# Token scales of five norms brought to all partitions by two DMAs through DRAM, and a gate chain moved by one unit

## The chip, the cores and the metric

One core of one Trainium2 chip runs the kernel. The metric is the device time of one execution in microseconds; for the kernel before it is the median of three runs, 1869.68 us (1867.63 to 1871.52).

## What is computed

A trunk of two layers on 512 tokens of width 1024, in float32. Each layer is half an FFN, a mixer, and half an FFN; each of these starts from a norm over the 1024 features of a token. The first mixer is forgetting attention, the second banded attention (windows of two chunks of 64 tokens) with sinks. A last norm follows.

```python
def rms_norm(x, g):
    xf = x.astype(F32)
    y = xf * lax.rsqrt(jnp.mean(xf * xf, axis=-1, keepdims=True) + RMS_EPS)
    return (y * g.astype(F32)).astype(x.dtype)

def swiglu(x, w_in, w_out):
    gate, up = jnp.split(x @ w_in, 2, axis=-1)
    return (jax.nn.silu(gate) * up) @ w_out

# forgetting attention: q, k, v, f_logit = split(u @ w_in)
    log_f = jax.nn.log_sigmoid((f_logit + b_f).astype(F32))
    c = jnp.cumsum(log_f, axis=1).transpose(0, 2, 1)
    s = s + cb[..., None] - c[:, :, None, :]
# banded attention: q, k, v = split(u @ w_in + b_in)

    for i in range(DEPTH):
        h = h + 0.5 * swiglu(rms_norm(h, norm_g[i, 0]), ffn_w_in[i, 0], ffn_w_out[i, 0])
        u = rms_norm(h, norm_g[i, 1])
        m = fox_mixer(u, ...) if kind == 0 else swa_mixer(u, ...)
        h = h + m
        h = h + 0.5 * swiglu(rms_norm(h, norm_g[i, 2]), ffn_w_in[i, 1], ffn_w_out[i, 1])
    return rms_norm(h, final_g)
```

## The kernel before

The residual `h` lies in SBUF with the features on partitions, 8 blocks of 128 features by 512 tokens. All products are split in three: a value is kept as a high part `_hi` (rounded) and the rest `_lo`, and a product is the matmuls hi x hi, hi x lo and lo x hi. ScalarE makes the high parts, VectorE the low ones, TensorE multiplies.

**Weights** come in units of 128 x 1024 values (512 KB), numbered through the whole program. SyncE loads them into a ring `raw` of four (`load`, L323 to L328): the load of unit n waits until unit n - 4 has been split (`w_ready`). ScalarE copies a unit into one of two `w_hi` slots once TensorE has used the unit two before (`split_next`, L1112 to L1119), VectorE makes `w_lo` (`split_lo`, L1546). A unit is 24 matmuls of 128 x 512.

**Norms** are numbered nn = 0 to 5 (FFN 0, forgetting attention 1, FFN 2 and 3, banded attention 4, FFN 5). The gain is put on `h` before the products, the scale of each token only after them, since it is a factor of a column. So a section starts with its first two units while the scale is being made: `token_sums` (L518) on TensorE, `mean_squares` (L1578) on VectorE, a power of -0.5 on GpSimd (`pow_rstd`, L453), which gives `rstd`, a token per partition, 128 x 4. What follows the products has the tokens along the row, and needs the scale as a row on all partitions, `rstd_row`. For this VectorE writes four diagonal matrices (`diagonals`, L1585), TensorE multiplies them by ones (`row_sums`, L524) into bank 5, and ScalarE copies it (`row_copy`, L1180).

**FFN** (`ffn`, `in_body`): a body is four units, two for 256 gate features (banks 0 and 1) and two for the same up features (banks 2 and 3). VectorE scales the gate by `rstd_row` (L1650), ScalarE applies SiLU (L1198), VectorE scales and multiplies the up half. TensorE's next body waits for the gate scaling (`gate_scaled`) before it takes banks 0 and 1 again. In the first body `row_sums` stands behind the third unit.

**Forgetting attention** (`fox`): unit 0 is V, unit 1 the gate logits (bank 4, 16 rows), then the rest of V (units with k = 1 to 7), with the first q and k between. The gate chain on VectorE and ScalarE (L1765 to L1818, L1320 to L1327) takes the logits, applies the row, and makes the running sum `decay`; it stands at k = 1 and 2. At k = 3 ScalarE and VectorE take the first four banks of V (`v_ready`), and TensorE's first q waits for bank 0 of them.

**Banded attention** (`window`): k and v units, then q of pair 0 and 1. `row_sums` stands after five of the eight steps of q's first unit. After the row VectorE scales k (L1951), q (L1948) and v (L1953); ScalarE and VectorE make the halves (L1440, L1423, L1431, L1909), then split the next weight unit (L1114, L1546). Then come the rounds of the head pairs: scores (L994), maxima (L1969), exponentials (L1473), normalizing (L2019), turning, values. `place_q` has SyncE move a q into place in every round, in the order of its loads.

The order on every engine is the order of the code.

Of the kernel before, what the change touches and what calls it, by code (L numbers as in the profile page):

```python
# [45 lines left out]
FIRST_AT = (11264, 10240)  # L46
LAST_PAIR = (KB // 2 - 1) * len(OUT_KBS)
# [30 lines left out]
def build(nc, x, gains, ffn_in, ffn_out, mix_w, fox_b, swa_bq, swa_bk, swa_bv, sinks, y):  # L78
    ctx = ExitStack()
    with ctx:  # L80
# [25 lines left out]
        diag = sb("diag", [P, SEQ])  # L106
        gain = sb("gain", [P, 7 * KB])
# [65 lines left out]
        row_ready = sem("row_ready")  # L173
        gate_scaled = sem("gate_scaled")
# [134 lines left out]
        def _(sp):  # L309
# [20 lines left out]
            def load_ffn(f):  # L330
# [22 lines left out]
                with sp.Fori(1, IN_BODIES) as i:  # L353
                    load_in(i)
# [16 lines left out]
            def load_window():  # L371

                for u in range(SWA_UNITS):
# [8 lines left out]
                    load((SWA_BASE + u) % RAW, mix_w[FOX_UNITS + u], UNIT, SWA_BASE + u - RAW + 1)  # L382

# [24 lines left out]
            load_ffn(0)  # L408
            load_fox()
            load_ffn(1)  # L410
            load_ffn(2)
            load_window()
            load_ffn(3)
# [77 lines left out]
        def _(pe):  # L491
# [30 lines left out]
            def row_sums(nn):  # L522
                pe.wait_ge(diag_ready, nn + 1)
# [76 lines left out]
            def ffn(f, nn):  # L600
                base = FFN_BASE[f]

                def in_body(i):
                    peeled = type(i) is int
                    for r in range(IN_UNITS):
# [17 lines left out]
                        if peeled and r == 2:  # L623
                            row_sums(nn)
# [202 lines left out]
            def fox(nn):  # L827
                n = FOX_BASE
                for k in range(V_UNITS):
# [4 lines left out]
                    if k == V_UNITS // 2:  # L834
                        pe.wait_ge(row_ready, nn + 1)
# [19 lines left out]
                    if k == 1:  # L855
                        row_sums(nn)
# [111 lines left out]
            def window(nn):  # L968
# [74 lines left out]
                row_sums(nn)  # L1043
# [63 lines left out]
        def _(act):  # L1107
# [70 lines left out]
            def row_copy(nn):  # L1178
                act.wait_ge(row_sum, nn + 1)
                act.activation(rstd_row[:, :], bank[5][:, :], ACT.Copy).then_inc(row_ready, 1)  # L1180

            def ffn(f, nn, last):
                base = FFN_BASE[f]

                def in_body(i):
                    for r in range(IN_UNITS):
# [6 lines left out]
                        if type(i) is int and r == 2:  # L1193
# [112 lines left out]
            def fox(nn):  # L1306
# [5 lines left out]
                row_copy(nn)  # L1312
                for k in range(1, V_UNITS):
                    step(n)
                    n += 1
                    if k == 1:
# [8 lines left out]
                    if k == 2:  # L1325
# [125 lines left out]
            def window(nn):  # L1451
# [5 lines left out]
                row_copy(nn)  # L1457
# [83 lines left out]
        def _(dve):  # L1541
# [84 lines left out]
            def ffn(f, nn, last):  # L1626
                base = FFN_BASE[f]

                def in_body(i):
                    first = type(i) is int  # L1630
                    for r in range(IN_UNITS):
# [7 lines left out]
                        if first and r == 1:  # L1639
                            if f == 0:  # L1640
                                first_mean_squares()
                            else:
                                mean_squares(nn, 5)
                            diagonals(nn)
                        if r == (2 if first else 1):
                            dve.wait_ge(unit_used, base + 4 * i + (3 if f == 0 and first else 2))
                            if first:
                                dve.wait_ge(row_ready, nn + 1)
# [105 lines left out]
            def fox(nn):  # L1754
# [7 lines left out]
                diagonals(nn)  # L1762
                dve.wait_ge(row_ready, nn + 1)
                dve.wait_ge(unit_used, FOX_BASE + 2)
                dve.tensor_tensor(x0, bank[4][0:HEADS, :], rstd_row[0:HEADS, :], ALU.mult).then_inc(f_chain, 1)  # L1765
                dve.wait_ge(f_chain, 1)
# [350 lines left out]
```

## Time and profile before

| | us |
|---|---|
| median of 3 runs | 1869.68 |
| the profiled execution | 1868.03 |
| its span, first to last instruction | 1866.2 |
| TensorE matmuls busy | 1849.2 (99%) |
| VectorE busy | 926.1 (50%) |
| ScalarE busy | 696.1 (37%) |
| DMA, mean of 16 engines | 97 GB/s |

The granted clock of TensorE is 0.999. The chain that ended last is followed back from the last instruction, at each step to what released it. A matmul of 128 x 512 is shown with 0.39 us, yet one begins every 0.23 us: matmuls overlap, so steps between starts are read rather than durations.

### The profile page before, as it was taken

To read this page: it belongs to the slowest core of one execution; us is meant where nothing else is said; L and a number is where in the kernel's file an instruction comes from. 1 tells how busy PE (TensorE), PEld (TensorE's weight loads), DVE (VectorE), ACT (ScalarE), POOL (GpSimd) and SP (SyncE) were. 2 spreads that over 40 slices of the span, in tenths; PEclk is the share of its full clock that TensorE was granted. 3 is DMA by queue.
4 is the path that set the end of the run, shared out by engine and by line. 5 is a ranking of instruction groups with operands and counts; after the bars stand their busy time and mean duration, and the time that the engine had idled before them with its cause. 6 is when DMAs were issued, how large, how long until landed. Compare 5 with 4: busy or idle time off the path is not lost.

```text
span 1866.2 us, 24031 instructions
## 1 busy us (share of the span) xinstructions
PE 1849.2 (99%) x8703; PEld 1522.8 (82%) x8703; DVE 926.1 (50%) x1337; ACT 696.1 (37%) x1149; POOL 24.7 (1%) x44
## 2 busy tenths in 40 slices
PE   9999999999999999999999999999999999999998
PEld 7888888877777888888888888888887888888888
DVE  5444434356887544444334444434379644444332
ACT  5232223245765432323323323323368433232332
POOL 1000000000000000000000000000000000000000
PEclk9999999999999999999999999999999999999999
DMA  4223223323332232222333232223322222222332
GB/s 170 101 91 101 87 89 105 119 95 107 86 94 67 94 102 91 100 97 81 110 107 106 96 101 90 96 88 108 122 79 70 91 93 98 99 92 90 96 104 84
DMA packets 59882, 181.85 MB, mean 97 GB/s; under 512 B 7472, under 2 KB 10032, under 8 KB 59824
## 3 DMA queue, kind: packets, MB, share of 16 engines
q1 hardware_dynamic: 59680, 181.05, 30.0%
q8 instruction: 36, 0.59, 0.1%
q14 instruction: 22, 0.18, 0.0%
q10 hardware_dynamic: 144, 0.03, 0.0%
HBM read 171.48 MB, written 2.10 MB: 93 GB/s over the span
## 4 chain that ended last, share of the span: by engine, by line
PE 94%; DVE 2%; ACT 2%; issue 1%; DMA 0%; POOL 0%; DVEq 0%; SPq 0%; ACTq 0%; POOLq 0%
PE bank L498 89%; PE bank L874 1%; PE bank L890 1%; ACT scratch L1473 0%; PE bank L906 0%; ACT wide_hi L1423 0%; DVE scratch L2019 0%; PE bank L994 0%; DVE w_lo L1546 0%; PE bank L524 0%; DVE wmax L1969 0%; ACT wide_hi L1279 0%; PE bank L565 0%; DVE wide_lo L1985 0%; DMA scratch<-x_dram 0%
## 5 line engine op out<-in xcount | busy, mean ns | idle before, releaser
L1546 DVE TENSOR_TENSOR w_lo<-raw,w_hi 128x1024 fp32r<-128x1024 f32 (+1 forms) x343 | 392.2, 1143 | 818.5 <-ACT w_hi L1114 817.4
L1114 ACT ACTIVATE w_hi<-raw 128x1024 fp32r<-128x1024 f32 (+1 forms) x343 | 341.1, 995 | 848.1 <-PE bank L498 841.4
L498 PE MATMUL bank<-u_hi,w_hi 128*128 128x512 f32 (+1 forms) x1592 | 630.3, 396 | 0.3 <-DVE w_lo L1546 0.3
L498 PE MATMUL bank<-u_hi,w_lo 128*128 128x512 f32 (+1 forms) x1592 | 620.2, 390 | 0.0
L498 PE MATMUL bank<-u_lo,w_hi 128*128 128x512 f32 (+1 forms) x1592 | 620.2, 390 | 0.0
L498 PEld LDWEIGHTS bank<-u_hi,w_lo 128*128 128x128 f32 (+1 forms) x1592 | 298.1, 187 | 63.9
L498 PEld LDWEIGHTS bank<-u_hi,w_hi 128*128 128x128 f32 (+1 forms) x1592 | 298.6, 188 | 61.0 <-issue 1.1
L498 PEld LDWEIGHTS bank<-u_lo,w_hi 128*128 128x128 f32 (+1 forms) x1592 | 298.5, 188 | 59.1 <-issue 1.0
L498 PE MATMUL bank<-wide_hi,w_hi 128*128 128x512 f32 (+1 forms) x812 | 314.7, 388 | 1.2 <-DVE w_lo L1546 1.1
L498 PE MATMUL bank<-wide_hi,w_lo 128*128 128x512 f32 (+1 forms) x812 | 313.1, 386 | 0.0
L498 PE MATMUL bank<-wide_lo,w_hi 128*128 128x512 f32 (+1 forms) x812 | 313.1, 386 | 0.0
L498 PEld LDWEIGHTS bank<-wide_hi,w_hi 128*128 128x128 f32 x812 | 152.5, 188 | 32.2 <-DVE w_lo L1546 1.3
L498 PEld LDWEIGHTS bank<-wide_hi,w_lo 128*128 128x128 f32 x812 | 152.5, 188 | 30.8
L498 PEld LDWEIGHTS bank<-wide_lo,w_hi 128*128 128x128 f32 x812 | 152.6, 188 | 29.7
L1204 ACT ACTIVATE wide_hi<-scratch 128x512 f32 (+1 forms) x88 | 54.4, 633 | 139.8 <-DVE scratch L1661 139.8
L1665 DVE TENSOR_TENSOR wide_lo<-scratch,wide_hi 128x512 f32 (+1 forms) x88 | 57.0, 689 | 12.9 <-ACT wide_hi L1204 12.5
L1650 DVE TENSOR_TENSOR scratch<-bank,rstd_row 128x512 f32<-128x512 f32 x88 | 56.3, 681 | 1.5 <-PE bank L571 1.5
L1661 DVE TENSOR_TENSOR scratch<-scratch 128x512 f32<-128x512 f32 x88 | 56.4, 682 | 0.0
L1655 DVE TENSOR_TENSOR scratch<-bank,rstd_row 128x512 f32<-128x512 f32 x88 | 56.3, 681 | 0.0
L1198 ACT ACTIVATE scratch<-scratch 128x512 f32<-128x512 f32 x88 | 50.3, 616 | 1.7 <-DVE scratch L1650 1.6
L1360 ACT ACTIVATE wide_hi<-bank 128x512 fp32r<-128x512 f32 (+1 forms) x64 | 28.1, 441 | 41.8 <-PE bank L890 41.6
L1129 ACT ACTIVATE u_hi<-h,gain (+1 forms) x40 | 28.6, 716 | 39.0 <-DVE h L1552 39.0
(210 smaller groups left out, 1246.9 us busy)
## 6 DMA issues: line engine op xcount, KB each, us to landing
raw<-ffn_in_dram SPq DMA_DIRECT2D x175, 512.0 KB, 3.2
raw<-ffn_out_dram SPq DMA_DIRECT2D x128, 384.0 KB, 3.0
raw<-mix_w_dram SPq DMA_DIRECT2D x51, 512.0 KB, 3.2
wide_hi<-wide_hi SPq DMA_DIRECT2D x28, 128.0 KB, 2.3
y_dram<-raw SPq DMA_DIRECT2D x8, 256.0 KB, 2.7
wide_lo<-wide_lo SPq DMA_DIRECT2D x14, 128.0 KB, 2.3
wide_hi<-wide_hi SPq DMA_DIRECT2D x7, 256.0 KB, 2.8
scratch<-x_dram SPq DMA_DIRECT2D x2, 512.0 KB, 7.1
```

Of the source, the lines that this page charges most:

```text
L498: mm = pe.matmul(out, a, b, start=first and k == 0, stop=last and k == n - 1)
L874: pe.matmul(out, part[:, q_at:q_at + P], part[:, k_at:k_at + nk], start=k == 0 and i > 0, stop=False)
L1114: act.activation(w_hi[:, slot, 0:cols], raw[:, (base + r) % RAW, 0:cols], ACT.Copy)\
L1129: act.activation(dyn(u_hi if nn < 6 else h, m_at), dyn(h, m_at), ACT.Copy, scale=gain[:, bass.ds(8 * nn + i4 + r, 1)]).then_inc(u_hi_ready, 1)
L1198: act.activation(silu_buf[:, c * SEQ:(c + 1) * SEQ], g_scaled_buf[:, c * SEQ:(c + 1) * SEQ], ACT.Silu)\
L1204: act.activation(dyn(wide_hi, 2 * SEQ * i + c * SEQ), up_buf[:, c * SEQ:(c + 1) * SEQ], ACT.Copy)\
L1360: act.activation(wide_hi[:, a:a + cols], bank[5 + at % 2][:, 0:cols], ACT.Copy)\
L1546: dve.tensor_tensor(w_lo[:, s, 0:cols], raw[:, r, 0:cols], f32(w_hi[:, s, 0:cols]), ALU.subtract).then_inc(w_ready, 1)
L1650: dve.tensor_tensor(g_scaled_buf[:, c * SEQ:(c + 1) * SEQ], bank[c][:, :], rstd_row[:, :], ALU.mult).then_inc(gate_scaled, 1)
L1655: dve.tensor_tensor(up_buf[:, c * SEQ:(c + 1) * SEQ], bank[2 + c][:, :], rstd_row[:, :], ALU.mult).then_inc(up_scaled, 1)
L1661: dve.tensor_tensor(up, up, silu_buf[:, c * SEQ:(c + 1) * SEQ], ALU.mult)\
L1665: dve.tensor_tensor(dyn(wide_lo, 2 * SEQ * i + c * SEQ), up_buf[:, c * SEQ:(c + 1) * SEQ], f32(dyn(wide_hi, 2 * SEQ * i + c * SEQ)), ALU.s ...
```

## The change

For the norms 1 to 5 the row is no longer made by diagonals, a matmul and a copy. SyncE writes `rstd` into a row of DRAM (128 partitions x 4 values, transposed by the access pattern), waits for it, and reads the row into all 128 partitions of `rstd_row`. In an FFN this stands behind the loads of the first two bodies, in a mixer behind the load of its eighth unit. The takers wait for `row_placed` in place of `row_ready`. Norm 0 stays as it is. In forgetting attention the gate chain moves by one unit: its first part is now at k = 1 behind the split, Exp, Ln and the sum at k = 2, the copy and the subtraction at k = 3. TensorE waits for `ms_ready` where it writes bank 5 again.

```diff
+            def place_row(nn):
+                count = 16 * ROW_MOVES[nn]
+                sp.wait_ge(rstd_ready, nn + 1)
+                sp.dma_start(row_dram.rearrange("o (t p) -> (o p) t", p=P), rstd[:, :], allow_slow_non_contiguous=True)\
+                  .then_inc(row_turned, 16)
+                sp.wait_ge(row_turned, count)
+                sp.dma_start(rstd_row[:, :], row_dram.to_broadcast([P, SEQ])).then_inc(row_placed, 16)
...
                 else:
                     load_in(0)
-                with sp.Fori(1, IN_BODIES) as i:
+                    load_in(1)
+                    place_row(nn)
+                with sp.Fori(1 if f == 0 else 2, IN_BODIES) as i:
...
+                    if u == RAW + 3:
+                        place_row(4)        # load_window; load_fox the same with place_row(1)
...
-                        if peeled and r == 2:
-                            row_sums(nn)
...
                     if k == V_UNITS // 2:
-                        pe.wait_ge(row_ready, nn + 1)
+                        pe.wait_ge(ms_ready, nn + 1)
                         pe.wait_ge(f_chain, 1)
...
                 f(5)
-                row_sums(nn)
+                pe.wait_ge(ms_ready, nn + 1)
                 f(KB + 2)
...
-                        if type(i) is int and r == 2:
+                        if f == 0 and type(i) is int and r == 2:
                             row_copy(nn)
...
-                row_copy(nn)
                 for k in range(1, V_UNITS):
                     step(n)
                     n += 1
-                    if k == 1:
+                    if k == 2:
...
-                    if k == 2:
+                    if k == 3:
                         act.wait_ge(f_chain, 7)
...
                 act.wait_ge(biases_ready, 1)
-                row_copy(nn)
...
                             if f == 0:
                                 first_mean_squares()
+                                diagonals(nn)
                             else:
                                 mean_squares(nn, 5)
-                            diagonals(nn)
...
+                            if first and f:
+                                dve.wait_ge(row_placed, 16 * ROW_MOVES[nn])
...
-                diagonals(nn)
                 dve.wait_ge(biases_ready, 1)
-                dve.wait_ge(row_ready, nn + 1)
+                dve.wait_ge(row_placed, 16 * ROW_MOVES[nn])
```

## Rows read from the trace of the kernel before

**Rows 1.** The page: busy time by engine, and the chain that ended last by engine.

```profile
PE 1849.2 (99%) x8703; PEld 1522.8 (82%) x8703; DVE 926.1 (50%) x1337; ACT 696.1 (37%) x1149; POOL 24.7 (1%) x44
...
PE 94%; DVE 2%; ACT 2%; issue 1%; DMA 0%; POOL 0%; DVEq 0%; SPq 0%; ACTq 0%; POOLq 0%
```

**Rows 2.** The chain by time (start, us, what), first and last of five L524.

```profile
388.83 0.86 PE bank L524 x2
...
1507.41 0.86 PE bank L524 x2
```

**Rows 3.** Timeline of TensorE at norm 3: start, us, engine, line, operation, tiles.

```profile
1004.44 0.40 PE L498 MATMUL bank<-u_hi,w_lo 128*128 128x512 f32 x1
1004.68 1.02 PE L524 MATMUL bank<-diag,ones 128*128 128x512 f32 x2
...
1005.77 0.40 PE L498 MATMUL bank<-u_lo,w_hi 128*128 128x512 f32 x1
```

**Rows 4.** Timelines of GpSimd, VectorE, TensorE and SyncE at norm 2.

```profile
640.02 1.00 POOL L453 TENSOR_TENSOR rstd<-ms,half 128x4 f32<-128x4 f32 x1 [82.97 <-DVE ms L1578]
...
646.12 1.28 DVE L1650 TENSOR_TENSOR scratch<-bank,rstd_row 128x512 f32<-128x512 f32 x2
...
650.04 0.39 PE L498 MATMUL bank<-u_hi,w_hi 128*128 128x512 f32 x1
...
639.97 6.75 SPq L328 DMA_DIRECT2D raw<-ffn_in_dram  x2
```

**Rows 5.** The page's DMA issues: count, KB each, median us to landing.

```profile
wide_hi<-wide_hi SPq DMA_DIRECT2D x28, 128.0 KB, 2.3
y_dram<-raw SPq DMA_DIRECT2D x8, 256.0 KB, 2.7
...
wide_hi<-wide_hi SPq DMA_DIRECT2D x7, 256.0 KB, 2.8
...
gain<-gains_dram ACTq DMA_DIRECT2D x1, 28.0 KB, 3.5
bf<-fox_b_dram SPq DMA_DIRECT2D x1, 0.1 KB, 8.3
```

**Rows 6.** The page's DMA queues: packets, MB, share of 16 engines' span.

```profile
q1 hardware_dynamic: 59680, 181.05, 30.0%
```

**Rows 7.** Timelines of GpSimd, ScalarE, VectorE and TensorE at norm 1.

```profile
383.61 2.34 POOL L453 TENSOR_TENSOR rstd<-ms,half 128x4 f32<-128x4 f32 x1 [354.81 <-DVE ms L1578]
...
392.34 1.28 ACT L1320 ACT_TABLE_LOAD   x1 [1.07 <-DVE scratch L1769]
...
400.65 1.06 ACT L1114 ACTIVATE w_hi<-raw 128x1024 fp32r<-128x1024 f32 x1 [1.08 <-PE bank L498]
...
396.33 0.68 DVE L1811 TENSOR_TENSOR scratch<-scratch 16x512 f32<-16x512 f32 x1 [2.60 <-ACT scratch L1323]
...
397.69 1.21 DVE L1815 TENSOR_TENSOR_SCAN scratch<-scratch 16x512 f32<-16x512 f32 x1
...
405.89 0.39 PE L498 MATMUL bank<-u_hi,w_hi 128*128 128x512 f32 x1
```

**Rows 8.** Timelines of GpSimd and VectorE at norm 4.

```profile
1362.02 1.01 POOL L453 TENSOR_TENSOR rstd<-ms,half 128x4 f32<-128x4 f32 x1 [11.56 <-DVE ms L1578]
...
1365.92 0.69 DVE L1951 TENSOR_TENSOR sq<-bank,rstd_row 128x512 f32<-128x512 f32 x1 [1.98 <-ACT rstd_row L1180]
1367.21 0.69 DVE L1948 SCALAR_TENSOR_TENSOR scratch<-bank,rstd_row 128x512 f32<-128x512 f32 x1 [0.60 <-PE bank L498]
...
1371.99 1.22 DVE L1546 TENSOR_TENSOR w_lo<-raw,w_hi 128x1024 fp32r<-128x1024 f32 x1 [0.54 <-ACT w_hi L1114]
1373.57 0.69 DVE L1969 TENSOR_REDUCE wmax<-bank 128x4 f32<-128x512 f32 x1 [0.35 <-PE bank L994]
```

**Rows 9.** The chain by time through banded attention, its first and last part.

```profile
1373.57 0.70 DVE wmax L1969
...
1448.06 1.24 DVE scratch L2019
```

More of the change, by code:

```diff
@@ L46 @@
 FIRST_AT = (11264, 10240)
+ROW_MOVES = {1: 1, 2: 2, 3: 3, 4: 4, 5: 5}
 LAST_PAIR = (KB // 2 - 1) * len(OUT_KBS)
@@ L106, in build @@
         diag = sb("diag", [P, SEQ])
+        row_dram = nc.dram_tensor("row_dram", (1, SEQ), F32, kind="Internal").ap()
         gain = sb("gain", [P, 7 * KB])
@@ L406, in load_fox @@
                     load((FOX_BASE + u) % RAW, mix_w[u], UNIT, FOX_BASE + u - RAW + 1)
-            load_ffn(0)
+                    if u == RAW + 3:
+                        place_row(1)
+            load_ffn(0, 0)
             load_fox()
-            load_ffn(1)
-            load_ffn(2)
+            load_ffn(1, 2)
+            load_ffn(2, 3)
             load_window()
-            load_ffn(3)
+            load_ffn(3, 5)
             for t in range(TB):
@@ L1641, in in_body @@
                                 first_mean_squares()
+                                diagonals(nn)
                             else:
                                 mean_squares(nn, 5)
-                            diagonals(nn)
                         if r == (2 if first else 1):
                             dve.wait_ge(unit_used, base + 4 * i + (3 if f == 0 and first else 2))
-                            if first:
-                                dve.wait_ge(row_ready, nn + 1)
+                            if first and f == 0:
+                                dve.wait_ge(row_ready, 1)
+                            if first and f:
+                                dve.wait_ge(row_placed, 16 * ROW_MOVES[nn])
                             for c in range(2):
@@ L1761, in fox @@
                 n += 1
-                diagonals(nn)
[L1763 to L1766, printed above, removed]
-                dve.tensor_scalar(x0, x0, bf[:, 0:1], None, ALU.add).then_inc(f_chain, 1)
-                dve.wait_ge(f_chain, 2)
-                dve.scalar_tensor_tensor(out=x1, in0=x0, scalar=-1.0, in1=x0, op0=ALU.mult, op1=ALU.max)\
-                   .then_inc(f_chain, 1)
-                dve.tensor_scalar(x3, x0, 0.0, None, ALU.min).then_inc(f_chain, 1)
                 def project_scaled(n, is_q, count):
@@ L1807, in fox @@
                     if k == 1:
+                        dve.wait_ge(row_placed, 16 * ROW_MOVES[nn])
+                        dve.wait_ge(unit_used, FOX_BASE + 2)
+                        dve.tensor_tensor(x0, bank[4][0:HEADS, :], rstd_row[0:HEADS, :], ALU.mult).then_inc(f_chain, 1)
+                        dve.wait_ge(f_chain, 1)
+                        dve.tensor_scalar(x0, x0, bf[:, 0:1], None, ALU.add).then_inc(f_chain, 1)
+                        dve.wait_ge(f_chain, 2)
+                        dve.scalar_tensor_tensor(out=x1, in0=x0, scalar=-1.0, in1=x0, op0=ALU.mult, op1=ALU.max)\
+                           .then_inc(f_chain, 1)
+                        dve.tensor_scalar(x3, x0, 0.0, None, ALU.min).then_inc(f_chain, 1)
+                    if k == 2:
                         dve.wait_ge(f_act, 2)
@@ L1937, in window @@
                 mean_squares(nn, 5)
-                diagonals(nn)
                 dve.wait_ge(biases_ready, 1)
-                dve.wait_ge(row_ready, nn + 1)
+                dve.wait_ge(row_placed, 16 * ROW_MOVES[nn])
                 def project_scaled(n, j):
```

12 lines of the change are left out of this document (6 added, 6 removed).

## The prediction

> **What bounds the kernel now.** I read the page's table of busy time and its chain that ended last first: TensorE is busy 99% of the span and carries 94% of the chain [rows 1]. So a microsecond that TensorE no longer issues is a microsecond of the span, unless something else becomes late. Next the chain in order of time: the matmul that turns the token scales into a row (L524) lies on it itself, five times after the first norm, 0.86 us each [rows 2]. The timeline of TensorE there shows the same from its own side: L524 begins at 1004.68, the second matmul behind it at 1005.77; the matmul before L524 began 0.24 us ahead of it, the usual step, so without L524 that second one would begin at about 1004.91, 0.86 us earlier [rows 3]. Last I read the other engines around each norm, since the new row comes from a longer way round: when the scales are ready, who takes the row, and when TensorE needs what the taker makes.
>
> **Removed.** Five of the six L524 matmuls: 5 x 0.86 = 4.3 us of TensorE's own path. Beside them go the diagonals on VectorE (four operations, 0.9 us) and the copy of the row on ScalarE (0.6 us). Neither engine is the bound there, so these count only where they lie ahead of the row. The norm of the first FFN keeps its matmul.
>
> **Added.** For each of the five norms SyncE waits for the scales, issues a write of them to DRAM (128 partitions, 4 values each, 512 single values in a transposed order), waits for it, and issues a read of the 2 KB row into all partitions (256 KB). I call S the time from the end of the power operation on GpSimd to the row on all partitions. The trace has neither move, so I bound them. Read: 128 KB landed in 2.3, 256 KB between SBUF places in 2.8, 256 KB to DRAM in 2.7 us [rows 5]; I take 2.8, and 2.3 to 3.5 as its bounds. Write: it cannot be under the 2.3 of the quickest row. The row nearest in kind is the gain load, 128 partitions with 224 bytes each, 3.5 us [rows 5]; I take that. The highest row is the load of 16 single values, 8.3 us, but it stood behind the loads at the start [rows 5]. With 0.1 us for the two starts on SyncE, S = 3.5 + 2.8 + 0.1 = 6.4 us; lowest 2.3 + 2.3 + 0.1 = 4.7; highest 8.3 + 2.8 + 0.1 = 11.2. The Trainium skill ("DMA: Bandwidth & Descriptors", Anatomy of one DMA) holds that a write to HBM waits longest for its receipt. The trace has 2.7 for DRAM against 2.8 for SBUF at 256 KB [rows 5], so the rule adds nothing here.
>
> SyncE's queue: what is queued behind place_row is the weight load after it. In the second FFN one load is issued at 639.97, and the next one ends its issue at 646.7, for it waits for the weight ring [rows 4]. With S's first part at 3.6 us from 641.02 SyncE is free at 644.6, ahead of that next issue. The loads are not late, and even 5 us more would cost nothing, since the ring is four units ahead of TensorE's use. The read is issued before the next load, so they do not collide.
>
> **The three FFN norms (2, 3, 5).** Scales ready at 641.02 (640.02 + 1.00); the taker is the gate scaling L1650, two operations, 1.28 us; it began at 646.12. TensorE needs its banks 0 and 1 back for the next body, whose first matmul began at 650.04 [rows 4]. Without L524 it would begin at 649.18. So the row must be there by 649.18 - 1.28 - 0.2 = 647.7, that is S up to 6.7. At S = 6.4 the row comes at 647.4, 1.3 us later for VectorE than before, and TensorE does not see it. Behind the gate scaling VectorE has the next split of weights, which it began only at about 651, so no harm there. Each norm gives its 0.86, less max(0, S - 6.7). The cover is 0.3 us: thin.
>
> **Forgetting attention (norm 1).** Scales ready at 385.95; the power operation took 2.34 here [rows 7]. The gate chain is shifted by one unit. Exp and Ln with their table loads took 3.95 us (392.34 to the release at 396.29), the sum and scan after them 2.6 (396.33 to 398.90) [rows 7]. Now Exp comes behind the split of one more unit. A unit is 24 matmuls of 0.23 us, 5.4; the one before that whose end ScalarE waited for at 400.65 ended at about 395.2, now 394.3, so its split ends at 395.4. The row plus 1.95 us of chain operations must be there by then: row by 393.5, S up to 7.5. The scan then ends at 395.4 + 3.95 + 2.6 = 402.0. The copy of its result (0.6), the first V half on ScalarE (0.6), and the subtractions on VectorE (0.7 each) bring the first V block to about 404.6. TensorE needs that block (its bank 0) at 405.89, now 405.03 [rows 7]. So the shift is covered by 0.4 us, and this norm gives 0.86 less max(0, S - 7.9). The shift moves no instruction onto TensorE.
>
> **Banded attention (norm 4).** Scales ready at 1363.03. Before, the row was taken at 1365.92 and the scaling of q, which waited for TensorE, began at 1367.21. From there to the end of the split L1546 (1371.99 + 1.22 = 1373.21) is a row of work on ScalarE and VectorE: q halves, a copy, the weight split, 6.0 us. Right behind it VectorE takes the first maximum, at 1373.57, which then waited 0.35 for TensorE's scores [rows 8]. Now q's scaling begins 0.7 us after the row (the scaling of k, 0.69), so the maximum cannot begin before row + 6.7. At S = 6.4 the row is there at 1369.4, the maximum at 1376.1, that is 2.5 us late; in general late by S - 3.8. TensorE's 0.86 is swallowed. Is the lateness given back? From this maximum to 1449.3 the chain that ended last runs through VectorE, ScalarE and one DMA, with short pieces of TensorE between [rows 9]; each round of a head pair starts from the last. I count the whole 2.5 us.
>
> **Sum.** T(S) = -4 x 0.86 + (S - 3.8) + 3 max(0, S - 6.7) + max(0, S - 7.9). S = 6.4: -3.44 + 2.6 = -0.9 us. S = 4.7: -2.5. S = 7.8: +3.9. S = 11.2: +20.8. The profiled execution took 1868.03 us (span 1866.2 and 1.8 around it), 1.65 under the median of 1869.68; so its span would be 1865.3, and the median 1869.68 - 0.9 = 1868.8.
>
> **Rivals.** (1) *The row is late for the gate banks.* If the write is paid by the element, TensorE waits at the second body of three FFNs. What a packet costs: 59,680 packets took 30.0% of 16 engines' 1866.2 us, 0.150 us each [rows 6]. 512 elements over 16 engines are 32 in a row, 4.8 us, on a fixed part of 1.8 (2.3 less the 0.5 that 128 KB more cost): write 6.6, S = 9.5, T = -3.44 + 5.7 + 8.4 + 1.6 = +12.3, time 1882. It decides from S = 7.8, a write of 4.9 us. Against it: the packets counted are mostly of kilobytes. The Trainium skill ("DMA: Bandwidth & Descriptors", Rules for kernel authors) speaks for this rival: a strided last dimension becomes one descriptor per element, and a plain copy with a rearranged pattern is no way to transpose. By its table of measured loads (section Bandwidth, about 10.5 ns a packet) 32 of them would be an estimated 0.3 us, and the sum would stay at the forecast or below. No row shows single values without other traffic.
> (2) *The window absorbs the lateness.* TensorE, VectorE and ScalarE are all nearly full there, and pieces of TensorE stand in the chain; if the rounds have slack, banded attention costs nothing and the time is 1869.7 - 3.4 = 1866.3. Against it: the first round is pure VectorE and ScalarE after the maximum.
> (3) *Near miss.* S between 6.7 and 7.8, for instance through the load of 512 KB issued 1.1 us ahead of the write: T from -0.5 to +3.9. S = 7.2 gives +1.5, time 1871.2.
>
> **How the numbers follow.** Forecast (S 4.7 to 6.7, T -2.5 to -0.5) 0.52; near miss 0.18; late for the banks 0.20; window absorbs 0.10. About 0.2% (3.7 us) is what a measurement of this kernel can tell from no change. Faster by that needs more than the four matmuls on the path give; it is left only where the window also gives its 0.86 (T = -4.3): half of rival 2, 0.05. Slower is rival 1 and the edge of rival 3: 0.21. Same: 0.74. The range reaches from 1866.5 (T = -3.2; rival 2's better half lies below) to 1878 (T = +8.3, S = 8.7; two thirds of rival 1 lie above).
>
> **What would show it.** In the profile after: no L524 behind 29.8 us; TensorE's first two bodies of an FFN without a wait between them; the DMA list gives the landing of both moves: write under 3.8 and read near 2.8; L1650 begins about 1.3 us later against the scales than before; in banded attention the first maximum of VectorE begins some 13 us after the scales instead of 11.5 (1363.03 to 1376.1 against 1373.57 before, less where TensorE is earlier), and the end of the section follows it. The prediction is wrong if the write lands later than 4.9 us, with waits of TensorE for L1650 in its list, or if the loads of SyncE become late, which would show as ScalarE waiting for raw.

## The result, and the profile after

| | before | after |
|---|---|---|
| median, us | 1869.79 (4 runs, 1867.63 to 1871.52) | 1910.97 (4 runs, 1910.81 to 1912.13) |
| profiled execution, us | 1868.03 | 1910.95 |
| its span, us | 1866.2 | 1909.2 |
| granted clock | 0.999 | 0.990 |

The ratio is 1.0222, with a 95% interval of 1.0204 to 1.0240: 41 us slower. The forecast was 1868.8 in a range of 1866.5 to 1878. In the medians below two executions that stood far outside are left out, 3810.71 us of e5 and 2553.42 us of e8. First the page of after: busy time and the chain that ended last by engine (against [rows 1]).

```profile
PE 1857.9 (97%) x8693; PEld 1529.1 (80%) x8693; DVE 921.4 (48%) x1317; ACT 694.0 (36%) x1144; POOL 24.5 (1%) x44
...
PE 89%; DMA 4%; DVE 3%; ACT 2%; issue 1%; POOL 0%; DVEq 0%; SPq 0%; ACTq 0%; POOLq 0%
```

And the two new moves in the list of DMA issues (count, KB each, median us to landing):

```profile
rstd_row<-row_dram SPq DMA_DIRECT2D x5, 256.0 KB, 5.0
row_dram<-rstd SPq DMA_DIRECT2D x5, 2.0 KB, 8.2
```

Ten matmuls fewer (8693 against 8703: each L524 was two records), and a DMA that had 0% of the chain has 4%. The write of 2 KB lands after 8.2 us (7.4 to 9.5), the read of 256 KB after 5.0 (4.0 to 5.6). The forecast had 3.5 and 2.8. The packets of SyncE's queue, against [rows 6]:

```profile
q1 hardware_dynamic: 63040, 182.37, 30.3%
```

These are 3360 more than before, 5 x (512 + 128 + 32): each write went out as one packet for each of its 512 values, each read as 128 packets of 2 KB, and each of the two moves has 16 small ones besides.

Next, norm 2 on each engine of after, in order of what causes what (against [rows 4]). The columns are start, duration, engine, line, operation, tiles, and in brackets the idle time ahead of it and what ended that. The power operation is now L472, the write L338, the read L341, the gate scaling L1665, the matmul L517.

```profile
646.73 1.01 POOL L472 TENSOR_TENSOR rstd<-ms,half 128x4 f32<-128x4 f32 x1 [82.98 <-DVE ms L1591]
...
647.76 0.38 SPq L338 DMA_DIRECT2D row_dram<-rstd  x1
657.24 0.32 SPq L341 DMA_DIRECT2D rstd_row<-row_dram  x1
...
661.36 1.29 DVE L1665 TENSOR_TENSOR scratch<-bank,rstd_row 128x512 f32<-128x512 f32 x2 [8.45 <-DMA rstd_row<-row_dram]
...
662.71 0.79 PE L517 MATMUL bank<-u_hi,w_hi 128*128 128x512 f32 x1 [6.72 <-DVE scratch L1665]
663.30 0.63 PE L517 MATMUL bank<-u_lo,w_hi 128*128 128x512 f32 x1
663.73 0.63 PE L517 MATMUL bank<-u_hi,w_lo 128*128 128x512 f32 x1
...
667.57 0.57 PE L517 MATMUL bank<-u_hi,w_lo 128*128 128x512 f32 x1
667.98 0.39 PE L517 MATMUL bank<-u_hi,w_hi 128*128 128x512 f32 x1
668.21 0.39 PE L517 MATMUL bank<-u_lo,w_hi 128*128 128x512 f32 x1
```

S, from the end of the power operation (647.74) to the row (661.36), is 13.6 us, not 6.4. TensorE stands 6.72 us for the gate scaling. Then something that the prediction did not have: the twelve matmuls from 662.71 on begin 0.43 us apart instead of 0.23. The granted clock says why, in windows over the same stretch (columns: busy time and count of each engine, granted clock, DMA share, GB/s).

```profile
650.00:656.00 6.00, 5.99 (x27) 4.63 (x25) 1.23 (x1) 2.35 (x2) 0.00 (x0) 1.00 0.00 0
656.00:659.00 3.00, 0.00 (x0) 0.00 (x0) 0.00 (x0) 0.00 (x0) 0.00 (x0) 1.00 0.09 20
659.00:662.00 3.00, 0.00 (x0) 0.00 (x0) 0.64 (x2) 0.00 (x0) 0.00 (x0) 0.85 0.80 240
662.00:663.00 1.00, 0.29 (x1) 0.29 (x2) 0.65 (x2) 0.91 (x2) 0.00 (x0) 0.50 0.01 4
...
667.00:668.00 1.00, 1.00 (x4) 0.72 (x4) 0.92 (x2) 0.65 (x2) 0.00 (x0) 0.53 0.84 332
668.00:670.00 2.00, 2.00 (x10) 1.67 (x9) 1.30 (x2) 0.59 (x1) 0.00 (x0) 1.00 0.14 57
```

The first line is about the write: from 650 to 656 it is under way (issued at 647.76, landed at 657.24), and the share of the DMA engines is 0.00. Its last packet ended 2.0 us after the issue; the other 7.5 us are a wait in which the trace records no packet. The same holds for the other four writes: the last packet ended 2.0 to 2.6 us after the issue, and from there to the landing it is 5.4 to 6.8 us.

The clock was at 1.00 when TensorE stopped, fell to 0.50 (1.2 instead of 2.4 GHz) in the wait, and was back at 1.00 at 668. From 662.71 to 667.98 are twelve steps in 5.27 us; at 0.227 each they would be 2.7. So 2.5 us are lost behind this wait, beside the wait itself; the same count behind the other four gives 2.0, 2.4 and 2.2 (norms 3, 4, 5) and 1.7 (norm 1, where the clock fell only after TensorE had resumed).

The waits of after for the whole span (total, times, longest) give the rest.

```profile
PE bank L517 <- DVE scratch L1665: 19.6, 3, 7.0
...
PE bank L517 <- DVE sq L1965: 10.4, 1, 10.4
```

The 10.4 us stand in banded attention; forgetting attention has two waits, of 3.67 and 0.55 us (timelines of VectorE, TensorE and ScalarE at norms 4 and 1, against [rows 8] and [rows 7]; L1983 is the first maximum, L1334 the Exp of the gate chain, L1840 the taking of V):

```profile
1399.40 0.69 DVE L1965 TENSOR_TENSOR sq<-bank,rstd_row 128x512 f32<-128x512 f32 x1 [13.42 <-DMA rstd_row<-row_dram]
...
1400.24 0.77 PE L517 MATMUL bank<-u_hi,w_hi 128*128 128x512 f32 x1 [10.44 <-DVE sq L1965]
...
1409.23 0.69 DVE L1983 TENSOR_REDUCE wmax<-bank 128x4 f32<-128x512 f32 x1 [3.15 <-PE bank L1009]
...
401.12 0.68 DVE L1815 TENSOR_TENSOR scratch<-bank,rstd_row 16x512 f32<-16x512 f32 x1 [8.77 <-DMA rstd_row<-row_dram]
...
403.28 1.20 DVE L1559 TENSOR_TENSOR w_lo<-raw,w_hi 128x1024 fp32r<-128x1024 f32 x1
...
404.54 0.50 PE L517 MATMUL bank<-w_hi,u_hi 128*128 128x512 f32 x1 [3.67 <-DVE w_lo L1559]
...
403.10 1.28 ACT L1334 ACT_TABLE_LOAD   x1 [6.56 <-DVE scratch L1819]
...
412.42 0.47 PE L517 MATMUL bank<-u_hi,w_hi 128*128 128x512 f32 x1 [0.55 <-DVE wide_hi L1840]
```

**Where the time went, section by section.** The starts of the power operation cut the span at the norms (before / after): 383.61 / 384.78, 640.02 / 646.73, 1001.01 / 1016.24, 1362.02 / 1385.58, 1503.58 / 1539.19, and 1841.86 / 1884.79 for the last norm. The first section has 1.2 us at the start of the span, before any part of the change (first power operation at 27.78 / 28.96). The others:

| section behind norm | longer by | wait of TensorE | half clock | L524 gone | sum |
|---|---|---|---|---|---|
| 1 | 5.5 | 3.7 + 0.55 | 1.7 | -0.9 | 5.0 |
| 2 | 8.5 | 6.7 | 2.5 | -0.9 | 8.3 |
| 3 | 8.3 | 7.0 | 2.0 | -0.9 | 8.1 |
| 4 | 12.1 | 10.4 | 2.4 | -1.0 | 11.8 |
| 5 | 7.3 | 5.9 | 2.2 | -0.9 | 7.2 |

Together 41.8 us longer, of which the terms give 40.4: nothing of size is missing. This is TensorE's own account, what it did with the time; for norm 1 it is not the account of causes, as the last part shows. What L524 gives is taken from [rows 2] and the first experiment below. What is open from here: why the row takes 13 us, whether the half clock is a cost of its own, and what the parts are worth without the late row.

### The profile page after: what moved, and what is told of

It reads as the page before. It is cut to its first block, busy times and chain, and to the rows that moved or that the text cites. A ratio compares the mean times of both kernels' runs of the same rounds, so it can differ in the third digit from the quotient of the medians.

```text
span 1909.2 us, 23954 instructions
## 1 busy us (share of the span) xinstructions
PE 1857.9 (97%) x8693; PEld 1529.1 (80%) x8693; DVE 921.4 (48%) x1317; ACT 694.0 (36%) x1144; POOL 24.5 (1%) x44
## 3 DMA queue, kind: packets, MB, share of 16 engines
q1 hardware_dynamic: 63040, 182.37, 30.3%
## 4 chain that ended last, share of the span: by engine, by line
PE 89%; DMA 4%; DVE 3%; ACT 2%; issue 1%; POOL 0%; DVEq 0%; SPq 0%; ACTq 0%; POOLq 0%
PE bank L517 85%; DMA row_dram<-rstd 2%; DMA rstd_row<-row_dram 1%; PE bank L889 1%; PE bank L905 1%; DVE w_lo L1559 1%; PE bank L921 0%; POOL rstd L472 0%; PE bank L1009 0%; ACT scratch L1486 0%; ACT wide_hi L1437 0%; ACT wide_hi L1294 0%; DVE scratch L2033 0%; PE bank L581 0%; ACT wide_hi L1374 0%
## 5 line engine op out<-in xcount | busy, mean ns | idle before, releaser
L517 PE MATMUL bank<-u_hi,w_hi 128*128 128x512 f32 (+1 forms) x1592 | 633.1, 398 | 30.9 <-DVE scratch L1665 19.6
L517 PE MATMUL bank<-u_lo,w_hi 128*128 128x512 f32 (+1 forms) x1592 | 623.5, 392 | 0.0
L517 PE MATMUL bank<-u_hi,w_lo 128*128 128x512 f32 (+1 forms) x1592 | 623.3, 392 | 0.0
L517 PEld LDWEIGHTS bank<-u_hi,w_hi 128*128 128x128 f32 (+1 forms) x1592 | 300.9, 189 | 93.5 <-DVE scratch L1665 21.3
L517 PEld LDWEIGHTS bank<-u_hi,w_lo 128*128 128x128 f32 (+1 forms) x1592 | 300.1, 189 | 64.5
L517 PEld LDWEIGHTS bank<-u_lo,w_hi 128*128 128x128 f32 (+1 forms) x1592 | 300.8, 189 | 58.9
L517 PE MATMUL bank<-wide_hi,w_hi 128*128 128x512 f32 (+1 forms) x812 | 314.7, 388 | 1.2 <-DVE w_lo L1559 1.0
L517 PE MATMUL bank<-wide_hi,w_lo 128*128 128x512 f32 (+1 forms) x812 | 313.1, 386 | 0.0
L517 PE MATMUL bank<-wide_lo,w_hi 128*128 128x512 f32 (+1 forms) x812 | 313.0, 386 | 0.0
L517 PEld LDWEIGHTS bank<-wide_hi,w_hi 128*128 128x128 f32 x812 | 152.5, 188 | 32.2 <-DVE w_lo L1559 1.3
L517 PEld LDWEIGHTS bank<-wide_hi,w_lo 128*128 128x128 f32 x812 | 152.5, 188 | 30.9
L517 PEld LDWEIGHTS bank<-wide_lo,w_hi 128*128 128x128 f32 x812 | 152.6, 188 | 29.7
L1665 DVE TENSOR_TENSOR scratch<-bank,rstd_row 128x512 f32<-128x512 f32 x88 | 56.4, 683 | 26.3 <-DMA rstd_row<-row_dram 24.8
L1144 ACT ACTIVATE u_hi<-h,gain (+1 forms) x40 | 28.7, 719 | 39.0 <-DVE h L1565 39.0
```

The costliest lines, as they stand in the source:

```text
L517: mm = pe.matmul(out, a, b, start=first and k == 0, stop=last and k == n - 1)
L1144: act.activation(dyn(u_hi if nn < 6 else h, m_at), dyn(h, m_at), ACT.Copy, scale=gain[:, bass.ds(8 * nn + i4 + r, 1)]).then_inc(u_hi_ready, 1)
L1665: dve.tensor_tensor(g_scaled_buf[:, c * SEQ:(c + 1) * SEQ], bank[c][:, :], rstd_row[:, :], ALU.mult).then_inc(gate_scaled, 1)
```

## The experiments

The theory (A) was: all of the loss is the late row, through TensorE's waits and the clock behind them; the removed matmuls give about 0.9 us each, and the moved gate chain costs nothing. Each ratio below is against the kernel before on the same chip, with its 95% interval.

**What the parts are worth without the row's way.** In e1 nothing moves a row: the takers wait for the scales alone and take the row of the first norm again (so the scales of norms 1 to 5 are left out of the result). All else is as after.

```diff
-                    place_row(nn)          # all three calls
-                                dve.wait_ge(row_placed, 16 * ROW_MOVES[nn])
+                                dve.wait_ge(rstd_ready, nn + 1)      # all three takers
```

> The change without its two moves: no row is made for norms 1 to 5; the takers wait for the token scales only and use the row that norm 0 left, so five norms use wrong scales. This is the change with a row that costs nothing and is never late. Theory A (the loss of 41 us is all lateness of the row, and the five removed matmuls are worth 0.86 us each): 4 to 5 us under the kernel before, ratio 0.9975, time about 1865; no wait of TensorE at the second body of an FFN and no fall of its clock. Rival B (the removed matmuls were cover for something else, such as the moved gate chain, so nothing is gained): ratio 1.000 or above.

Measured 1864.66 us against 1869.63, ratio 0.9973 (0.9962 to 0.9983). GpSimd's power operations in e1:

```profile
385.52 2.34 POOL L467 TENSOR_TENSOR rstd<-ms,half 128x4 f32<-128x4 f32 x1 [354.80 <-DVE ms L1586]
641.03 1.00 POOL L467 TENSOR_TENSOR rstd<-ms,half 128x4 f32<-128x4 f32 x1 [82.96 <-DVE ms L1586]
...
1361.25 1.01 POOL L467 TENSOR_TENSOR rstd<-ms,half 128x4 f32<-128x4 f32 x1 [11.57 <-DVE ms L1586]
1501.76 1.01 POOL L467 TENSOR_TENSOR rstd<-ms,half 128x4 f32<-128x4 f32 x1 [139.50 <-DVE ms L1586]
```

From 385.52 to 641.03 are 255.51 us, before 256.41: the matmul and nothing else. From 1361.25 to 1501.76 are 140.51, before 141.56: a window that gives its matmul too. Five sections give 4.7 us. That is the most that the change could have brought.

**The gate chain alone.** e2 keeps the matmul for every norm and only shifts the chain.

```diff
+MOVED = ()          # no norm's row goes through DRAM; chain at k = 1, 2, 3 as after
```

> Only the gate chain of forgetting attention is moved by one unit; all rows are made by diagonals, matmul and copy as before. Theory A (the move is covered): ratio 1.000, within 1 us of the kernel before. Rival C (the moved chain delays the first V bank by itself and holds part of the 5.5 us that norm 1 lost): 2 to 5 us slower, with a wait of TensorE near 406 us.

Measured 1869.01 against 1869.63, ratio 0.9997 (0.9988 to 1.0006). The section behind norm 1 took 256.57 (385.23 to 641.80) against 256.41. The shift costs nothing that can be seen.

**Banded attention apart.** e3 is after with norm 4 by its matmul, e4 is before with norm 4 alone by the two moves.

```diff
+MOVED = (1, 2, 3, 5)      # e3
+MOVED = (4,)              # e4, gate chain where it was
```

> The change with banded attention's norm (4) back to the matmul; norms 1, 2, 3, 5 by the two moves. Theory A (each norm pays alone): norm 4 lost 12 us in the trace of the change, so 12 us under the change, about 1899, ratio to before 1.0157. Rival D (the loads pushed back by the moves or the fallen clock carry over from one norm to the next): the saving differs from 12 us by more than 2.

> The kernel before with banded attention's norm (4) alone by the two moves. Theory A: 12 us slower than before, about 1882, ratio 1.0064; TensorE waits about 10 us for the scaling of k, which frees the bank of the second q unit, and then runs some 5 us at the half clock. My prediction's step (the late part is the first maximum of VectorE): with S of 12.8 it would be 9 us, and the wait would stand at the first scores instead.

e3: 1898.29, ratio 1.0158 (1.0142 to 1.0173). e4: 1881.41, ratio 1.0060 (1.0045 to 1.0076). The waits of e4 name the bank of the second q unit:

```profile
PE bank L520 <- DVE sq L1984: 11.3, 1, 11.3
```

e4 costs 11.8 and e3 28.7 over before, together 40.5 of the 41.2: the costs add up, and neither part hides the other. In e4 the one write took 9.5 us and the one read 4.0, so five of them in a kernel are not what makes them long.

**Is it the single values?** e5 writes the same 2 KB as 128 runs of 16 bytes, a partition's four values side by side; the scales then stand in the wrong order of tokens, all else is as after. e10 writes 256 runs of 8 bytes.

```diff
-    sp.dma_start(row_dram.rearrange("o (t p) -> (o p) t", p=P), rstd[:, :], ...)
+    sp.dma_start(row_dram.rearrange("o (p t) -> (o p) t", p=P), rstd[:, :], ...)              # e5
+    sp.dma_start(row_dram.rearrange("o (t p two) -> (o p) t two", p=P, two=2), ...)           # e10
```

> The change with the write in runs of 16 bytes (a partition's 4 scales side by side in DRAM, 128 runs) in place of 512 single values; the row then has its tokens in a wrong order, so five norms use wrong scales. Theory E (the write's 8.2 us are paid by the single values): the write lands in about 3.5 us, S falls from 13.4 to 8.7, and five norms give up 4 to 5 us each: 20 to 25 us under the change, about 1888. Rival F (the write's cost is a fixed one of small writes to DRAM, or waiting behind the load ahead of it): 7 to 8 us as before, time within 5 us of the change.

> The change with the write in 256 runs of 8 bytes (tokens in a wrong order in the row, so wrong scales). The write landed in 2.5 us with 128 runs of 16 bytes and in 8.2 with 512 single values. If every run costs the same, 5.7 us for 384 more runs, the write lands in 4.4 us; S about 8, TensorE waits 1 to 2 us at each gate bank, time 1880 to 1886. If only single values of 4 bytes are slow: write 2.5 to 3, time about 1872, as with runs of 16. If anything under 16 bytes is slow: write about 8, time about 1911.

e5: 1871.94, ratio 1.0018 (1.0008 to 1.0028). e10: 1880.60, ratio 1.0058 (1.0043 to 1.0074). The two moves in the DMA issues of e5 and TensorE's wait, then the same of e10:

```profile
rstd_row<-row_dram SPq DMA_DIRECT2D x5, 256.0 KB, 3.5
row_dram<-rstd SPq DMA_DIRECT2D x5, 2.0 KB, 2.5
```

```profile
PE bank L517 <- DVE sq L1965: 4.2, 1, 4.2
```

```profile
rstd_row<-row_dram SPq DMA_DIRECT2D x5, 256.0 KB, 4.7
row_dram<-rstd SPq DMA_DIRECT2D x5, 2.0 KB, 3.7
```

```profile
PE bank L517 <- DVE sq L1965: 6.5, 1, 6.5
PE bank L517 <- DVE scratch L1665: 5.0, 3, 1.7
```

The same bytes take 2.5 us in 128 runs, 3.7 in 256, and 8.2 in 512: 9 ns for each run more in the first step, 18 in the second. One line of access pattern was worth 39 of the 41 us.

Where these microseconds pass is in the traces too. SyncE's queue moved 61120 packets in e5, 61760 in e10 and 63040 in after, against 59680 before: one packet for each run of a write. But in all three the last packet of a write has ended 1.7 to 3.0 us after its issue. From there to the landing it is 0.4 to 1.3 us in e5, 1.4 to 1.9 in e10 and 5.4 to 7.5 in after. So the price is not paid by packets standing in line on the DMA engines, but behind the last one; what happens there no trace shows. The number of runs, their length, and how closely values of different partitions lie together in DRAM changed at once, and none was varied alone, so which of them is paid for stays open.

I had expected e5 near 1888; it went lower because S falls to 6.2 at norm 2 (641.29 to 647.48), under the cover, and there neither the wait nor the half clock comes. What is left of e5 is first banded attention: from 1360.50 to 1507.76 are 147.26 us, 5.7 over before, of which 4.2 are the wait above and 2.3 the clock (eleven steps from 1368.97 to 1373.77), less the matmul. The rest is not the row's: the section behind norm 1 took 257.03 us against 255.51 in e1, and the 1.5 us between them arise some 200 us behind the norm, where the granted clock fell to 0.50 (582 to 584 us) and matmuls of 128 x 512 began 0.43 us apart, behind waits of 1.1 and 0.7 us that stand in e1 too, without a fall.

**Why the read takes 5.0.** e6 reads 128 different rows of `x` in place of one row 128 times (so the scales of norms 1 to 5 are left out). e8 puts both moves one weight load earlier in SyncE's queue, so that no load is issued just ahead of the write.

```diff
-                sp.dma_start(rstd_row[:, :], row_dram.to_broadcast([P, SEQ])).then_inc(row_placed, 16)
+                sp.dma_start(rstd_row[:, :], x[0:P, 0:SEQ]).then_inc(row_placed, 16)            # e6
...
+                        if type(i) is int and i == 1 and r == IN_UNITS - 1:
+                            place_row(nn)                                                         # e8
```

> The change with the read taking 128 different rows of 2 KB (from the input x) in place of one row 128 times; the norms use wrong scales. Theory G (the read's 5.0 us come from 128 partitions reading the same 2 KB): it lands in about 2.8 us, as other moves of 256 KB, and the time is 5 x 2.2 = 11 us under the change, about 1900. Rival H (any read that size there takes 5.0): the same time as the change.

> The change with both moves one load earlier in SyncE's order: ahead of the 512 KB load that was issued about 1 us before the write (that load now waits behind the moves). Theory I (the write stands behind that load in the DMA queues): the write lands 1 to 3 us sooner, and the time is 5 to 15 us under the change. Rival (the load has landed by then or does not matter): the write stays at 7.4 to 9.5 us and the time within 2 us of the change, unless the pushed-back load itself is late, which ScalarE would show as waiting for raw.

e6: 1903.51, ratio 1.0184 (1.0167 to 1.0201). e8: 1911.86, ratio 1.0236 (1.0216 to 1.0257). The moves of e6, then of e8:

```profile
rstd_row<-x_dram SPq DMA_DIRECT2D x5, 256.0 KB, 4.0
row_dram<-rstd SPq DMA_DIRECT2D x5, 2.0 KB, 8.5
```

```profile
rstd_row<-row_dram SPq DMA_DIRECT2D x5, 256.0 KB, 5.8
row_dram<-rstd SPq DMA_DIRECT2D x5, 2.0 KB, 8.0
```

The load ahead does not lengthen the write: 8.0 without it, 8.2 with it. That theory fell. In e8 all 512 packets of a write have ended by 1.3 us after its issue, 0.7 to 1.3 us sooner than in after, and it still lands only after 7.9 to 9.4.

Every read of e6 is shorter than the one of after at the same norm, by 0.7 to 1.6 us, in the median 4.0 against 5.0. How much of that is the price of reading one row 128 times is not shown, since the rows of e6 are also not ones that were written just before. What makes up the rest stays open. The held-up weight load that goes out behind the read is not enough to explain it: at norm 2 of after that load is issued 0.7 us behind the read (L341 at 657.24, the load L332 at 657.92 in SyncE's timeline) and the read took 4.0, the quickest of the five, while at norm 4 no load is issued for 11 us and it took 4.6. With no load near, norm 4's read took 4.6 in after, 4.0 in e4, 4.4 in e10 and 3.4 in e5; with a load 0.4 us behind it, in e8, it took 5.5. So both the kind of write ahead and a load behind go with a longer read, and neither was tried alone.

**Is the half clock a cost of its own?** e7 keeps TensorE at work through the gate's wait with 28 matmuls of zeros in bf16 into an unused bank. The two moves stay as in after.

```diff
+                        if peeled and r == 3:
+                            for _ in range(28):
+                                pe.matmul(bank[6][:, :], warm[:, 0:P], warm[:, :], start=True, stop=True)
```

> The change with 28 matmuls of zeros (128x512, bf16, into a free bank) put at the end of the first body of FFN 1, 2 and 3, where TensorE would wait 6 to 7 us for the gate bank. Theory A (TensorE waits, its granted clock falls to half for the first 12 matmuls after the wait, which costs 2.4 us a time): the filled wait keeps the clock at full, three norms give up 2.4 us each, 7 us under the change, about 1904. Rival (the slow matmuls after the wait have another cause, for instance the arriving weight loads): the same time as the change or a little more.

Measured 1902.52, ratio 1.0186 (1.0169 to 1.0203), 8.4 us under after. TensorE's timeline in e7 at norm 2:

```profile
655.21 5.99 PE L644 MATMUL bank<-warm 128*128 128x512 bf16 x27
...
661.04 0.50 PE L517 MATMUL bank<-u_hi,w_hi 128*128 128x512 f32 x1
661.38 0.40 PE L517 MATMUL bank<-u_lo,w_hi 128*128 128x512 f32 x1
661.62 0.40 PE L517 MATMUL bank<-u_hi,w_lo 128*128 128x512 f32 x1
```

The real matmuls now begin 0.24 us apart from the second on, the granted clock does not fall at these three norms, and their sections are shorter than in after by 3.2, 2.3 and 2.0 us (norms 2, 3 and 5). The row came at S = 12.8, 13.6 and 12.9 against 13.6, 13.9 and 12.8 in after; without that difference 2.4, 1.9 and 2.1 are left, against 2.5, 2.0 and 2.2 counted above. At these norms the clock behind a wait is paid on top of the wait.

**Can the idea be had?** Runs of 16 bytes need the sums of a partition to be those of four neighbouring tokens. e9 gets this by TensorE's sums taking every fourth column of `acc` as weights, for norms 2, 3 and 5; norms 1 and 4 keep their matmul and the chain its place.

```diff
+MOVED = (2, 3, 5)
...
-                    mm = pe.matmul(bank[b][:, 2 * t:2 * t + 2], acc[:, t * P:(t + 1) * P], ones[:, 0:2],
+                    of = by_four[:, :, t] if nn in MOVED else acc[:, t * P:(t + 1) * P]
+                    mm = pe.matmul(bank[b][:, 2 * t:2 * t + 2], of, ones[:, 0:2],
```

> The kernel before with the two moves for the FFN norms 2, 3 and 5 only; there the token sums take every fourth token as weights, so that a partition holds four neighbouring tokens and the write goes out in runs of 16 bytes in the right order. Norms 1 and 4 by the matmul, the gate chain in its old place. Theory A with E (write about 2.5, read about 3.5, S about 6.1, under the 6.7 that TensorE can wait for): 3 x 0.86 = 2.6 us under the kernel before, ratio 0.9986, no wait for the gate bank. Rival (weights read with a step cost TensorE more, or the cover of 0.6 us is gone in some norm): ratio 1.000 or above.

Measured 1868.99 against 1869.69, ratio 0.9997 (0.9988 to 1.0006). The token sums of norm 2 before and in e9:

```profile
637.29 0.95 PE L518 MATMUL bank<-ones,acc 128*128 128x2 f32 x8
```

```profile
637.41 1.80 PE L542 MATMUL bank<-ones,acc 128*128 128x2 f32 x8
```

The row came in time (gate scaling at 647.30, no wait of TensorE for it), but the eight small matmuls took 0.85 us more with strided weights, just what L524 had cost. e11 therefore leaves the matmuls alone and has VectorE lay out `acc` by every fourth token as it adds.

```diff
+                    by_four = acc[:, :].rearrange("p (t f) -> p t f", t=TB)
+                    dve.tensor_tensor(by_four, by_four, sq[:, r % 2, :].rearrange("p (f t) -> p t f", t=TB), ALU.add)
```

> As the run with norms 2, 3 and 5 by the two moves in token order, but the token sums read plain weights again: the sum of squares is laid out by every fourth token where VectorE adds it up, for these three norms. In that run the eight small matmuls of the token sums took 1.80 us in place of 0.95, which gave back the 0.86 of the row's matmul. Theory A: they take 0.95 again, VectorE's additions stay at about 0.69 us, and the time is 3 x 0.86 = 2.6 us under the kernel before, ratio 0.9986. Rival (something else takes the place of the removed matmul, or reading with a step slows VectorE): ratio 0.9995 or above.

Measured 1868.07 (11 runs) against 1868.99, ratio 0.9997 (0.9988 to 1.0006). The groups of additions in e11 (count, busy, mean ns), and its chain by time behind forgetting attention:

```profile
L1596 DVE TENSOR_TENSOR acc<-acc,sq 128x512 f32<-128x512 f32 x24 | 26.0, 1085 | 0.0
...
L1599 DVE TENSOR_TENSOR acc<-acc,sq 128x512 f32<-128x512 f32 x22 | 15.1, 686 | 0.8 <-ACT sq L1158 0.5
```

```profile
602.45 1.10 DVE acc L1596
...
604.12 1.07 DVE acc L1596
605.19 1.15 DVE w_lo L1573
```

Strided, an addition takes 1.09 in place of 0.69 us, and behind forgetting attention, where VectorE is behind, two of them stand in the chain: the section behind norm 1, unchanged otherwise, took 257.00 against 256.41. The sections behind norms 2, 3 and 4 give 0.3, 0.9 and 0.2 (360.69, 360.14 and 141.35, against 360.99, 361.01 and 141.56). With the 0.8 of the last and less the 0.6 lost behind norm 1 that is 1.6 us between the two profiled executions, 0.9 between the medians, and not to be told from no change. No version that computes the norms beat before by more than can be measured.

## Why the prediction was wrong, point by point

**The step that failed is the term S.** The write was forecast at 3.5 us from the gain load [rows 5], 128 partitions with 224 bytes each; it measured 8.2. The read was forecast at 2.8 and measured 5.0. S was 12.8 to 14.0 in place of 6.4, above even the highest bound of 11.2. The choice of the row was the error: the gain load shares the number of partitions with the write, but the write has 512 pieces, and e5 and e10 show that with 128 and 256 pieces it would have landed in 2.5 and 3.7. The row that was set aside, 16 single values in 8.3 us behind the loads at the start, was nearer in time, but by luck: its reason (traffic ahead) isn't the write's, as e8 shows. The prediction also gave the landing of a write nothing of its own, from moves of 256 KB (2.7 for DRAM, 2.8 for SBUF); here 5.4 to 7.5 of each write's time lie behind its last packet.

**Rival 1 had the right symptom and the wrong place for the cost.** It had the write paid by the element at 6.6 us and TensorE waiting for the gate banks three times, 1882 us, with a chance of 0.20. The waits came, and the write does take longer the more pieces it has. But the 4.8 us that the rival puts on the DMA engines, 32 elements in a row on each, worked out from packets of kilobytes, are not there: in e8, with no load ahead, the 512 packets all started within 0.4 us. The wait behind them is what the rival lacked, and the write took 1.6 us more than it had.

The rule of the Trainium skill that it named ("DMA: Bandwidth & Descriptors", Rules for kernel authors: a strided last dimension becomes one descriptor per element) is borne out, if a packet is read as a descriptor: the count of packets rose by one for each of the 512 values. The price of about 10.5 ns for a packet in the Trainium skill ("DMA: Bandwidth & Descriptors", Bandwidth) gives an estimated 0.34 us for 32 packets on each engine, and the trace agrees as far as the packets go (the 0.4 us of e8). As a price of the whole write, which is how the prediction weighed it, it fails: going from 128 runs to 512 is 24 packets more for each of 16 engines, an estimated 0.25 us by it, and 5.7 us were measured.

**The sum with the measured S.** With the five values of S (14.0, 13.6, 13.9, 12.8, 12.8) the formula gives -3.4 + 9.0 + (6.9 + 7.2 + 6.1) + 6.1 = +32. So the mis-sized term explains three quarters of the 41.8 us of the sections. The rest is two terms that were missing. (At S = 6.4 the sum itself is -0.84, written as -0.9, which changes nothing.)

**Missing: the clock behind a wait.** At norms 2, 3, 4 and 5 each wait of TensorE has some ten matmuls at half speed behind it, which cost 2.5, 2.0, 2.4 and 2.2 us. Shown by the granted clock, and by e7 for the three FFN norms; for norm 4 it is counted and not tried. Every rival with a wait of TensorE in it lacked this term; at the forecast S it would have been nothing for the FFN norms.

**Missing: a second wait in banded attention.** The prediction named the first maximum of VectorE as what is late (S - 3.8). What comes first is TensorE: the second q unit needs the bank that the scaling of k frees, and it waited 10.4 us at S = 12.8, 4.2 at S = 6.6 in e5 and 6.5 in e10, where S is 8.9 (1365.20 to 1374.09): in all three S - 2.4. The path that was named is there as well, only shorter: by it the maximum could have begun at row + 6.7 = 1406.1, and it began at 1409.23, after 3.15 us of waiting for TensorE's scores. So the norm would have cost time even at S = 6.4, 4.0 of wait and 2.4 of clock, less its matmul: +5.4 instead of the +2.6 in the sum, which puts the forecast's own case 2.0 us over before, not 0.9 under. So even with S as forecast the change would not have come out faster. e5 is nearly that case, and lies 2.9 over (1871.94 against 1869.02), with the 1.5 us of the clock in forgetting attention in it.

**Norm 1: the mechanism was right.** The prediction had the first V block come through the gate chain, late from S = 7.9, which at 14.0 gives 6.1 us. The matmul that needs it began at 412.42, which is 411.25 without the 1.17 us by which the whole section stands later; the prediction had 405.03 for it without L524. That is 6.2 us late. The chain that ended last runs there through the gate chain, from L1819 over Exp and Ln (L1334, L1337), the scan (L1830) and the taking of V (L1840), and not through TensorE; its last pieces there (start, us, what):

```profile
411.53 0.76 DVE wide_hi L1840
...
412.42 3.68 PE bank L517 x15
```

In every run with the shifted chain and a late row this matmul begins 11.3 us behind the row, whatever TensorE met before: 401.12 to 412.42 in after, 399.02 to 410.33 in e6, 394.53 to 405.83 in e10. What the prediction did not name is that the weight split (403.28), which stands behind the wait for the row on VectorE's own queue, comes late too, and TensorE stood 3.67 us for it, with 1.7 us of half clock behind. These two, with the 0.55 at V, add up to 5.9 us, the same lateness met in three pieces: with the split in time, TensorE would have stood for all of it at V (not tried by a run, but in e6, at S = 12.1, the two waits are 1.74 and 2.12 with the clock at full between them, 3.9 in all, where S - 7.9 is 4.2).

**Right.** A removed matmul is worth 0.87 to 1.05 us wherever the row is in time (e1), banded attention included. The cover of the gate banks, forecast at S = 6.7: TensorE waited 6.7, 7.0 and 5.9 us at S = 13.6, 13.9 and 12.8, and 1.5 in e10 at S = 8.45 (641.15 to 649.60), each time S - 6.9, and not at all at 6.2 in e5. The shifted chain costs nothing (e2). The loads did not become late for ScalarE, though at norms 1, 2, 3 and 5 SyncE issued the next one only behind the read, where the prediction had it free in time: the only waits of ScalarE for `raw` in after, 3.0 and 1.7 us, stand in before with 3.1 and 1.6. "The window absorbs", rival 2, is refuted by e4.

## What to carry to other kernels

Before a matmul that makes a row is given up for a trip through DRAM, count the runs of the write, not its bytes or its partitions: with one run for each partition this one landed in 2.5 us, with four in 8.2. And wherever TensorE is the bound, price a wait as its length plus what the clock takes afterwards, unless TensorE would have to wait for another engine behind it anyway, as at norm 1. List for every new wait of an engine all that is queued behind it there, and all the banks that it holds.

## What the runs showed of the hardware that was not expected

- A DMA of 2 KB from 128 partitions to a row of DRAM landed in 2.5 us as 128 runs of 16 bytes, 3.7 as 256 of 8, 8.2 as 512 of 4. The difference lies behind the last packet: 0.4 to 1.3, 1.4 to 1.9 and 5.4 to 7.5 us from there to the landing, with no packet on the DMA engines.
- A read of one 2 KB row, just written, into 128 partitions took 5.0 us where 128 other rows took 4.0, both behind a slow write; behind a quick one (e5) it took 3.5.
- Behind waits of 3.7 to 11.3 us TensorE ran 8 to 14 matmuls of 128 x 512 at 1.2 GHz, 1.7 to 2.9 us lost each time; the loss does not follow the length of the wait (2.5 behind 6.7, 2.4 behind 10.4, 2.9 behind 11.3 in e4, 2.7 behind 6.5 in e10). Behind one of 1.5 us (e10, norm 2, matmuls from 650.94, 651.28, 651.51, 651.74) it lost nothing, yet in e5 the clock fell once where the longest wait was 1.1 us.
- Eight small matmuls with float32 weights of every fourth column took 1.80 us in place of 0.95; a float32 addition of 128 x 512 on VectorE with every fourth element, 1.09 in place of 0.69.
